# High parts ahead of exponentials on ACT, and the gates of an even attention opened in two batches

## What is computed

```python
def even_layer(x, g_norm, w_in, b_f, w_out):
    z = rms_norm(x, g_norm) @ w_in
    ...
    ya = forgetting_attention(hA(qa), hA(ka), hA(va), log_f).reshape(Bsz, S, WIDTH_FOX)
    yb = dilated_attention(hB(qb), hB(kb), hB(vb)).reshape(Bsz, S, WIDTH_DIL)
    y = jnp.concatenate([ya * jax.nn.silu(ga), yb * jax.nn.silu(gb)], axis=-1)
    return x + y @ w_out
...
    q, kc, vc, ks, vs, kw, vw, gates, u, bg, cg = jnp.split(z, offsets, axis=-1)
    kc_c = compress(kv(kc), cmp_pos[0], cmp_w1[0], cmp_b1[0], cmp_w2[0], cmp_b2[0])
    vc_c = compress(kv(vc), cmp_pos[1], cmp_w1[1], cmp_b1[1], cmp_w2[1], cmp_b2[1])
    o_cmp, p_cmp = cmp_attention(q, kc_c, vc_c)
    o_sel = sel_attention(q, kv(ks), kv(vs), idx)
    o_win = win_attention(q, kv(kw), kv(vw))
    o_attn = g[0] * o_cmp + g[1] * o_sel + g[2] * o_win
    o_conv = short_conv(u, bg, cg, conv_w)
    return jnp.concatenate([o_attn, o_conv], axis=-1) @ w_o
```

## Time and profile before

| | |
|---|---|
| median of 3 runs | 1506.97 us (1506.56 to 1507.9) |
| the profiled execution | 1507.06 us, its span 1504.9 us |
| mean granted clock of PE | 0.962 |
| busy PE, DVE, ACT | 92%, 65%, 50% of the span |

### The profile page before, as it was taken

One profiled execution on the slowest core, in us unless ns is written; L12 is line 12 of the kernel. 1 busy time (PEld: TensorE's weight loads), 2 busy tenths in 40 slices (PEclk: granted clock), 3 DMA queues, 4 the chain that ended last, 5 costly groups with the idle time before them and its releaser, 6 DMA issues.

```text
span 1504.9 us, 22452 instructions
## 1 busy us (share of the span) xinstructions
PE 1382.6 (92%) x9010; PEld 1230.8 (82%) x9010; DVE 981.1 (65%) x1354; ACT 756.0 (50%) x913; POOL 99.8 (7%) x112
## 2 busy tenths in 40 slices
PE   5999999999999887788999998698799999999995
PEld 5998988789988786678999887686688788888884
DVE  5446456565765566466544466566688889898887
ACT  3455467334323246433433326642377677677672
POOL 0000022100002110000222010001100000000000
PEclk9999999999999989899999999898699999999998
DMA  6543433446533543224654544413398998998995
GB/s 246 182 165 131 149 114 113 168 154 215 192 140 115 207 168 141 98 106 150 214 184 180 196 159 162 159 61 119 142 360 321 349 338 309 354 340 339 329 336 224
DMA packets 43673, 305.82 MB, mean 203 GB/s; under 512 B 4864, under 2 KB 5120, under 8 KB 7744
## 3 DMA queue, kind: packets, MB, share of 16 engines
q1 hardware_dynamic: 41328, 295.69, 53.3%
q0 software_dynamic: 2256, 8.88, 1.7%
HBM read 303.51 MB, written 1.05 MB: 202 GB/s over the span
## 4 chain that ended last, share of the span: by engine, by line
PE 68%; DVE 11%; ACT 9%; issue 6%; DMA 4%; POOL 1%; DVEq 0%; POOLq 0%; SPq 0%; ACTq 0%
PE g_ps L555 16%; PE g_ps L557 15%; PE g_ps L556 15%; ACT w_hi L1164 5%; PE a_ps L555 4%; DMA raw<-w_dram 4%; PE a_ps L557 4%; PE a_ps L556 4%; PE a_ps L560 4%; DVE w_lo L1486 3%; PE a_ps L564 2%; PE o_ps L560 2%; ACT prob L1196 2%; DVE tiny L1533 1%; DVE x L1617 1%
## 5 line engine op out<-in xcount | busy, mean ns | idle before, releaser
L1486 DVE TENSOR_TENSOR w_lo<-raw,w_hi 128x2048 fp32r<-128x2048 f32 x240 | 549.1, 2292 | 298.2 <-ACT w_hi L1164 292.2
L1164 ACT ACTIVATE w_hi<-raw 128x2048 fp32r<-128x2048 f32 x240 | 459.3, 1914 | 228.0 <-PE a_ps L557 78.9
L555 PE MATMUL g_ps<-w_hi,x_hi 128*128 128x256 f32 (+1 forms) x720 | 246.9, 343 | 17.9 <-DVE x_lo L1583 13.0
L555 PE MATMUL g_ps<-x_hi,w_hi 128*128 128x256 f32 x880 | 252.9, 287 | 0.0
L556 PE MATMUL g_ps<-x_lo,w_hi 128*128 128x256 f32 x880 | 250.0, 284 | 0.0
L557 PE MATMUL g_ps<-x_hi,w_lo 128*128 128x256 f32 x880 | 249.9, 284 | 0.0
L557 PE MATMUL g_ps<-w_hi,x_lo 128*128 128x256 f32 (+1 forms) x720 | 241.5, 335 | 0.0
L556 PE MATMUL g_ps<-w_lo,x_hi 128*128 128x256 f32 (+1 forms) x720 | 241.0, 335 | 0.0
L555 PEld LDWEIGHTS g_ps<-x_hi,w_hi 128*128 128x128 f32 x880 | 170.0, 193 | 4.6 <-issue 4.3
L556 PEld LDWEIGHTS g_ps<-x_lo,w_hi 128*128 128x128 f32 x880 | 170.0, 193 | 0.0
L557 PEld LDWEIGHTS g_ps<-x_hi,w_lo 128*128 128x128 f32 x880 | 169.8, 193 | 0.0
(11 more groups left out here) (285 smaller groups left out, 1994.5 us busy)
## 6 DMA issues: line engine op xcount, KB each, us to landing
raw<-w_dram SPq DMA_DIRECT2D x279, 1024.0 KB, 4.9
arena<-rows_dram POOLq DMA_DIRECT2D x3, 1024.0 KB, 5.7
x<-x_dram SPq DMA_DIRECT2D x2, 512.0 KB, 6.9
extra<-extra_dram POOLq DMA_DIRECT2D x1, 1024.0 KB, 5.5
extra<-rows_dram POOLq DMA_DIRECT2D x2, 512.0 KB, 4.1
y_spare<-rows_dram POOLq DMA_DIRECT2D x4, 256.0 KB, 4.6
out_dram<-x SPq DMA_DIRECT2D x2, 512.0 KB, 2.7
extra<-gains_dram SPq DMA_DIRECT2D x1, 512.0 KB, 4.7
```

What stands on the lines that cost most here:

```text
L555: pe.matmul(ps, lh, rh, start=start, stop=False, skip_group_check=True)
L1164: act.activation(w_hi[w_place(s)][:, :], raw[PLACE[s]][:, :], ACT.Copy).then_inc(hi_done, 1)
L1486: dve.tensor_tensor(w_lo[w_place(s)][:, :], raw[PLACE[s]][:, :], w_hi[w_place(s)][:, :].bitcast(F32), ALU.subtract).then_inc(lo_done, 1)
```

## The change

1. **ACT's loop** calls `between(i - 1)` ahead of the exponentials, in all four attentions.
2. **Gates.** A gate slot is copied out raw (Copy in the place of Silu). After the fourth and the eighth one instruction puts Silu over four gates in place (2048 columns, `gates_open`). DVE's products follow by a table (GATED): units 0 and 1 in step 4 of `between`, then 2, 3, none, 4, 5, 6 in steps 5 to 10, and 7 at the end as before.
3. **Sparse input slots** come in the order values, I_KC, first queries, keys, second queries. PE no longer waits for the second queries' copy ahead of the loop but in step 3.
4. **Compressed keys and values** are made by DVE at the head of its step 5, ahead of that step's maxima, in the place of the end of it.
5. **The convolution's split** stands on ACT ahead of, and on DVE ahead of, the part of the last slot I_B + 1 (both halves together); the first output slot moves from step 10 to step 9, ahead of the transposes of the compressed block.

```diff
-I_KC, I_Q, I_KS, I_W1, I_U, I_C, I_B = 1, 2, 4, 5, 9, 11, 13
+I_KC, I_Q, I_KS, I_W1, I_U, I_C, I_B = 1, (2, 4), 3, 5, 9, 11, 13
...
-        STEP_ROWS, STEP_GELU, STEP_KV, STEP_TAPS, STEP_PARTS, STEP_OUT = 2, 3, 4, (6, 7), (8, 9), (10, 11)
+        STEP_GELU, STEP_KV, STEP_TAPS, STEP_OUT = 3, 4, (6, 7), (9, 11)
...
+        GATE_STEPS = (3, 7)
+        GATED = [(), (), (), (), (0, 1), (2,), (3,), (), (4,), (5,), (6,)]
...
-                for s in (s0 + I_KC, s0 + I_Q):
+                for s in (s0 + I_KC, s0 + I_Q[0]):
                     rows_slot(s)
                 fold_rows(l)
-                for s in (s0 + I_Q + 1, s0 + I_KS):
+                for s in (s0 + I_KS, s0 + I_Q[1]):
...
                     if i == STEP_GELU:
+                        s = s0 + I_Q[1]
+                        pe.wait_ge(g_free[s % 3], g_nth[s] + 1)
                         turn_rows()
...
-                for s in (s0, s0 + I_Q, s0 + I_Q + 1, s0 + I_KS):
+                for s in (s0, s0 + I_Q[0], s0 + I_KS):
...
+                    if i:
+                        between(i - 1)
                     if i < len(jobs):
                         exps(i, 0)
                     if 2 <= i < len(jobs) + 2:
                         copy_odd(i - 2)
                     if i < len(jobs):
                         exps(i, 1)
-                    if i:
-                        between(i - 1)
...
-                    ins = act.activation(gate_even(s - EV_G[0]), g_ps[s % 3][:, :], ACT.Silu)
+                    ins = act.activation(gate_even(s - EV_G[0]), g_ps[s % 3][:, :], ACT.Copy)
...
-            attention(pairs_even(1), 8, lambda i: even_slot(24 + i) if i < 8 else ahead(EV_OUT + i - 8))
+            def gates_and_out(i):
+                if i < 8:
+                    even_slot(EV_G[0] + i)
+                else:
+                    ahead(EV_OUT + i - 8)
+                if i in GATE_STEPS:
+                    s = EV_G[0] + i
+                    act.wait_ge(g_free[s % 3], g_nth[s] + 1)
+                    four = arena[:, 512 * (i - 3):512 * (i + 1)]
+                    act.activation(four, four, ACT.Silu).then_inc(gates_open, 1)
+
+            attention(pairs_even(1), 8, gates_and_out)
...
-                copy_slot(s0 + I_Q + 1, sq[:, 2:4, :])
                 s = s0 + I_KS
                 act.wait_ge(used, s + 1)
                 for g in range(NKV):
@@ -1335,6 +1349,7 @@
                                              ACT.Copy)
                 ins.then_inc(g_free[s % 3], 1)
                 ahead(s)
+                copy_slot(s0 + I_Q[1], sq[:, 2:4, :])
...
+                        if m == I_B + 1:
+                            for j in range(2):
+                                act.wait_ge(g_free[(s0 + I_B + j) % 3], g_nth[s0 + I_B + j] + 1)
+                                act.activation(y_hi[:, 4 + 2 * j:6 + 2 * j, :],
+                                               part[:, j, :].rearrange("p (a b) -> p a b", a=2), ACT.Copy).then_inc(c_hi, 1)
...
+                    if i in before:
+                        before[i]()
...
-                s = EV_G[0] + u
-                dve.wait_ge(g_free[s % 3], g_nth[s] + 1)
+                dve.wait_ge(gates_open, u // 4 + 1)
...
-                    if i < 4:
-                        even_y(i, oT)
                     ahead(EV_G[0] + i)
                 else:
                     ahead(EV_OUT + i - 8)
-                if i in (5, 7, 9):
-                    even_y((i + 3) // 2, oT2)
+                for u in GATED[i]:
+                    even_y(u, oT if u < 4 else oT2)
...
-                    if i == STEP_KV:
-                        j, _ = kv_turn(l)
...
+                def keys_and_values():
+
+                    j, _ = kv_turn(l)
+                    dve.wait_ge(kv_full, l + 1)
+                    dve.tensor_scalar(kc2[:, :], g_ps[j][:, 0:30], vec[:, V_B2K + l:V_B2K + l + 1], None,
+                                      ALU.add).then_inc(kc_done, 1)
...
-                attention(pairs_sparse(l), A_L[l], None, between)
+                attention(pairs_sparse(l), A_L[l], None, between, {STEP_KV + 1: keys_and_values})
...
-        w.append(in_slots(np.concatenate([vs, vw, kc, vc, q, ks, kw], 1)))
+        w.append(in_slots(np.concatenate([vs, vw, kc, vc, q[:, :256], ks, kw, q[:, 256:]], 1)))
```

More of the change, by code:

```diff
@@ L1323, in _ @@
                 act.activation(xs[:, :, 0, :], xc_all, ACT.Copy).then_inc(xc_hi_done, 1)
-                copy_slot(s0 + I_Q, sq[:, 0:2, :])
+                copy_slot(s0 + I_Q[0], sq[:, 0:2, :])
                 act.wait_ge(rows_folded, l + 1)
@@ L1368, in between @@
                         ahead(s0 + m)
-                    if i in STEP_PARTS:
-                        j = STEP_PARTS.index(i)
-                        s = s0 + I_B + j
-                        act.wait_ge(g_free[s % 3], g_nth[s] + 1)
-                        act.activation(y_hi[:, 4 + 2 * j:6 + 2 * j, :], part[:, j, :].rearrange("p (a b) -> p a b", a=2),
-                                       ACT.Copy).then_inc(c_hi, 1)
                 def group_copy(g):
@@ L1709, in select, with attention @@
                         dve.tensor_scalar(sel[:, t, e, :], iota, r, None, ALU.is_equal).then_inc(m_sel, 1)
-            def attention(jobs, a0, group_out, between):
+            def attention(jobs, a0, group_out, between, before={}):
                 most, total = tiny[:, 0:16], tiny[:, 16:32]
@@ L1954, in _ @@
                 dve.tensor_tensor(xs[:, :, 1, :], xc_all, xs[:, :, 0, :].bitcast(F32), ALU.subtract).then_inc(xc_split, 1)
-                for m in range(I_Q, I_W1):
+                for m in range(I_Q[0], I_W1):
                     ahead(s0 + m)
```

30 lines of the change are left out of this document (14 added, 16 removed).

## The result

The changed kernel takes 1459.6 us (median of 1455.1, 1459.4, 1459.8 and 1460.6), the kernel before on the same chip 1507.4 (four runs, 1506.6 to 1509.9). The ratio is 0.9674, 95% interval 0.9651 to 0.9697: faster by 3.3%, some 47.8 us by the medians. The forecast was 1455.2, with a range of 1446 to 1468; the time lies in the range, 4.4 us above the forecast. The profiled execution took 1455.06 us, with a span of 1453.2. The kernel before ran again beside the experiments, with medians of 1506.8 to 1507.4. One run of one kernel (experiment 8) took 1697.6 us at a mean granted clock of 0.75; nothing here explains it, and its ratio leaves it out.

A forecast was written before the change was run, and what follows sets the result against it. PE, busy in 92% of the span, bounds the kernel, so only its waits and lost clock can be won. 7.2 + 44.6 = 51.8 us off 1507.06 gives 1455.3, by the median 1455.2; range 1446 to 1468.

The forecast's parts named there:

- Part 1: Second even attention: stalls of 8.4 us go, new waits cost 1.2, net 7.2 us off.
- the new wait at the end: End of second even attention: wait of 2.1 us (bounds 1.5 and 4.0) for GpSimd's unit 6, replacing 0.9.
- the ring: Loop step: ACT's exponentials, DVE's maxima, w_lo and w_hi wait in a circle, 9 us and more against PE's 8.40.
- rival B: Second even attention: each table switch costs 2.66 us, not 1.28; transposes wait 1.6; 1456.8 us; chance 0.05.
- Part 2: Each sparse layer: waits and lost clock go, 22.3 us off (bounds 16 and 25.7), two layers 44.6.
- (a): Sparse layer start: waits of 2.8, 1.4, 0.4 and 1.7 of clock go; new wait 3.4 with 1.6 of clock.
- (b): Sparse step 3: wait of 2.9 for hidden rows' copy and 1.7 of clock go; new probT wait 0.4.
- (c): Sparse step 5: w_lo finds w_hi done, keys and values ready 1.1 us early; 9.0 wait and 2.9 clock go.
- (d): Sparse layer tail: output slot covers the 2.1 wait; wait of 1.8 replaces 2.3; 2.3 of clock goes.
- A: Sparse layers: a late raw-tile landing beyond 1.1 us slack brings back keys' wait; partly 1463 to 1478, all 1479; chance 0.13.
- D: All four attentions: w_hi ahead of exponentials waits for its raw tile; slower, 1513 us at 12.5 landing; chance 0.03.
- C: Loop steps: w_hi starts no earlier, DVE's rest sets the ring, waits change names; 1504 to 1507 us; chance 0.02.

The follow-up runs named there:

- experiment 8: Changed kernel with a Silu for each gate and one w_lo of each sparse layer behind the first maxima: 1450.9 us, ratio to before 0.9619.
- experiment 1: Kernel before with only ACT's slot work (copy or Silu, then w_hi) moved ahead of the exponentials in all four attentions: 1475.5 us, ratio 0.9781.
- experiment 5: Changed kernel with the gates' edit undone (a Silu for each gate, no batches, products at their old steps): 1457.6 us, ratio to before 0.9668.
- experiment 6: Changed kernel with the gate products of units 5 and 6 one step earlier: 1456.8 us.
- experiment 9: Changed kernel with the order of its sparse input slots undone (queries, queries, keys): 1460.5 us, ratio to before 0.9678.
- experiment 10: Changed kernel with the sparse tail undone (convolution's parts behind w_hi and w_lo, output slots back in steps 10 and 11): 1462.9 us, ratio 0.9700.
- experiment 4: Changed kernel with DVE's keys and values put back to the end of step 4, behind that step's w_lo: 1473.1 us.
- experiment 3: Changed kernel with ACT's slot work put back behind the exponentials in all four attentions: 1480.9 us.
- Experiment 11: Changed kernel with the w_hi ahead of step 3's exponentials written three times in each sparse layer, ACT 3.86 us later: 1466.9 us.
- experiment 7: Changed kernel with one w_lo of each sparse layer moved behind the first maxima: 1452.9 us, ratio to before 0.9635.
- experiment 12: Kernel of experiment 8 with ACT's exponentials and probT copy ahead of w_hi in step 2 of each sparse layer: 1459.2 us.

## Why the prediction was right, point by point

**The place of the gain.** Right: but for 2.7 us of difference in stretches without an edit, it is all in the second even attention and the two sparse layers, 49.0 us against the 51.8 of the sum. The first even attention gave nothing, as forecast (192.75 and 192.93 at the first mark).

**Part 1, 7.2 us forecast, 5.2 measured: a term of the sum was mis-sized.** The stalls were worth 8.6 (experiments 1, 5 and 6), the forecast had 8.4. The failed term is the new wait at the end, "a wait of 2.1 (bounds 1.5 and 4.0)" in place of 0.9 and no clock behind it. It is 2.73, and clock goes with it. Windows of PE in the changed kernel (stretch, length, PE busy, PEld, DVE, ACT, POOL busy, granted clock, DMA share, GB/s):

```profile
284.95:288.70 3.75, 3.75 (x10) 2.94 (x11) 2.16 (x1) 0.00 (x0) 0.00 (x0) 0.54 0.22 57
288.70:292.60 3.90, 3.90 (x19) 3.19 (x17) 0.00 (x0) 0.20 (x1) 0.00 (x0) 1.00 0.62 248
```

3.75 x 0.46 = 1.7 us of clock; 2.73 - 0.94 + 1.7 = 3.5 us, where 1.2 was counted. The 2.3 us between them are the miss of part 1 (8.6 - 3.5 = 5.1, measured 5.2). Part 1 gives no reason for leaving the clock out. The rows of before had only shown that waits up to 1.7 us kept it, which does not bear a wait of 2.1. The other part is the wait itself, 2.73 and not 2.1: on POOL both parts of unit 6 run beside DVE's last product and low part, 1.42 and 1.60 us, where they took 1.04 and 1.30 for unit 5 (timeline of POOL):

```profile
281.80 1.42 POOL L483 TENSOR_TENSOR y_hi<-part,zero_col 128x512 fp32r<-128x512 f32 x1 [4.09 <-DVE part L1857]
283.30 1.60 POOL L486 TENSOR_TENSOR y_lo<-part,y_hi 128x512 fp32r<-128x512 f32 x1
```

**And a step of part 1 was wrong in its reason, though not in its number.** The forecast put the stalls' end down to both edits, the order and the 12.8 us of table loads that ACT is spared. The loads weren't needed: with 15 of them in the stretch E is 8.6 us shorter (experiments 1 and 5). ACT has time for them once `w_hi` stands first; what the ring could not bear was `w_hi` behind exponentials that wait for DVE's maxima. The batches alone brought 1.9, and on top of the order they cost 3.4.

**The table switch (rival B).** The forecast took 1.28 us for a load, no drain. The changed kernel's ACT in the first batch's step (timeline) has Silu 1.30 us after its load's start and the exponential 1.29 after the next, so the trace of after agrees with the earlier trace rows. The Trainium skill, "ScalarE: Activation LUTs", section "What ACT_TABLE_LOAD costs", counts 2.66 with a drain; neither trace shows one:

```profile
224.85 1.28 ACT L1283 ACT_TABLE_LOAD   x1
226.15 1.92 ACT L1283 ACTIVATE arena<-arena 128x2048 f32<-128x2048 f32 x1
228.09 1.28 ACT L1200 ACT_TABLE_LOAD   x1
229.38 0.40 ACT L1200 ACTIVATE prob<-prob,stat 128x128 f32<-128x128 f32 x1
```

The Silu over 2048 columns took 1.92 us, forecast 1.9, and PE waited for nothing in that step: probT was ready at 230.74, and the next transposes came at 231.59.

**Part 2, 22.3 us a layer forecast, 21.5 and 22.4 measured.** (a) The start: a wait of 3.4 forecast, 3.45 measured; clock 1.6 forecast, 4.42 x 0.39 = 1.7 by this window of the changed kernel:

```profile
568.46:572.88 4.42, 4.42 (x25) 3.32 (x25) 2.69 (x15) 4.42 (x14) 0.00 (x0) 0.61 0.53 222
```

What the slots' new order was worth, 2.8 + 1.7 + 1.4 + 0.4 - 3.4 - 1.6 = 1.3 by the forecast's numbers, was 0.1 and 0.6 (experiment 9). (b) Right: the hidden rows' wait is gone, and 0.3 for probT stands where 0.4 was forecast. (c) Right in the outcome: DVE finished keys and values 1.1 us before PE wants the bank (about 600.1), and stood idle for PE ahead of them. One clause was wrong: the `w_lo` ahead of them did not find its `w_hi` done, it stood 2.63 us for it. That cost nothing, as PE's product came 0.62 us later still (timeline of DVE):

```profile
594.76 2.29 DVE L1500 TENSOR_TENSOR w_lo<-raw,w_hi 128x2048 fp32r<-128x2048 f32 x1 [2.63 <-ACT w_hi L1168]
597.67 0.25 DVE L2024 TENSOR_SCALAR extra<-g_ps,vec 128x30 f32<-128x30 f32 x1 [0.62 <-PE g_ps L562]
597.84 1.18 DVE L2028 TENSOR_TENSOR arena<-g_ps,vec 32x128 f32<-32x128 f32 x4
```

(d) A wait of 1.8 forecast, 1.7 measured, and 0.6 more ("issue") ahead of the compressed block's values, which the forecast did not have. The clock stayed at 1.00 behind the 1.7, as forecast for a wait of that size; experiment 10 shows that the size of one wait does not decide it alone.

Which edit brought a layer's 21.9 us (mean of both): ACT's order 12.3 (experiment 1: 10.1 + 1.3 and 10.4 + 2.7), the keys' line 7.2 (experiment 4), the tail 1.7 (10), the slots' order 0.1 to 0.6 (9); the first was measured by adding it to the kernel before, the others by taking them from the changed one. That makes 21.3 to 21.8. But this says only that the last three hardly cover for each other. Taken out of the changed kernel, the order is worth less: 5.5 + 1.7 and 7.2 + 3.4, on the mean 8.9 (experiment 3). So 3.4 of its 12.3 come with the other edits too. Experiments 1 and 3 show most of the overlap: the order takes 4.2 us off the wait for the keys' line, and that line in its new place stays at 0 and 0.7 us even without the order. Likewise in the even attention: the order brings 8.6 put in alone, and costs 3.4 taken out.

**The rivals.** A did not come about. Experiment 11 shows that with ACT 3.86 us late its wait for the keys' line does not come about either; in place of its 1.1 us of slack, PE pays in step 3 for what lies beyond 0.3 us there. D's mechanism (a landing in front of exponentials) is real, `w_hi` stands 4.04 and 0.96 us for its transfer at 582.10 and 585.45 of the changed kernel, but PE waits only 0.3. It is what experiments 7, 8 and 12 ran into. B is answered above, and C fell with experiment 1: DVE's idle time for `w_hi` went from 21.9 to 7.8 us.

**The rest.** By stretches the forecast was 2.8 us too good: 2.0 in the even attention, 0.8 in the sparse layers. The profiled run's own time, 1455.06, is on the forecast only because its unedited stretches were 2.7 us shorter than before's.

## What to carry to other kernels

Where an engine both prepares a later step's data and finishes this step's chain, put the preparation first if its inputs are there, and look at how long the next engine stands for it; busy time that is taken off an engine with slack is worth nothing (the table loads, once the order was right). When work is gathered into a batch, cost the last consumer: what moved to a later step has less cover behind it, and price its wait with clock behind it, unless the trace shows a wait of that size that is free of it and no second wait close by (1.59 and 0.75 us with 1.5 us between them cost 1.6). When edits overlap, measure each by putting it in and by taking it out: the two differed here by 3.4 us a layer. And cut a run into stretches between marks of the program: here they mostly repeat within 0.2 to 0.5 us (once each 1.4 and 1.5), where whole runs of one kernel differ by 5.

## What the hardware showed beside this

Runs of one kernel differ by some 5 us (1455.1 to 1460.6 for the changed one), and the profiled runs differ in stretches that no edit touches. Up to the first scores of the second even attention the profiled runs took 192.75 to 196.35 us, and the feed-forward part between the two sparse layers 200.3 to 203.7, with PE's waits there alike (6.7 us for `x_lo`). The granted clock differs: from 40 to 80 us it is 0.96 in the changed kernel and 0.91 in experiment 6, both with PE busy throughout. That the before and the changed profile both have the short first stretch is luck, and in a comparison of 2 us it would mislead.

POOL's first part of a gate's product, which adds a column of zeros to one tile, took 1.04 us alone and 3.01 us when it started with a `w_lo` of DVE (experiment 5, timeline of POOL, where DVE's `w_lo` runs from 204.96 for 2.28 us):

```profile
205.14 3.01 POOL L483 TENSOR_TENSOR y_hi<-part,zero_col 128x512 fp32r<-128x512 f32 x1 [183.37 <-DVE part L1853]
```

It ends some 0.9 us after the `w_lo`, nearly its whole duration alone. The Trainium skill, "SBUF — State Buffer", section "SBUF: two separate sides", has a DVE instruction with two SBUF inputs and a GpSimd instruction that reads SBUF share one pair of ports, as an exclusive lock that whichever starts first holds for its whole instruction. Here DVE started first, with two inputs in SBUF, and this row agrees with that.
